# Twelve projection slots of a two-block network: high and low activations in one matmul of 512 columns, added on eviction

## The reference, cut to what matters

```python
for l in range(2):
    x = x + 0.5 * swiglu(rms_norm(x, norm_ffn1[l]), ffn1_wi[l], ffn1_wo[l])
    h = rms_norm(x, norm_mix[l])
    p = h @ w_in[l]                      # 1024 -> 2688 columns: the mixing slots
    p_a, p_q, p_k, p_v, p_c = jnp.split(p, split_pts, axis=-1)
    y_a, v_first = rwkv7_mixer(p_a, v_first, ...)
    y_b = chunk_attention(p_q, p_k, p_v, ...)
    y_c = multiscale_pool(p_c, ...)
    x = x + jnp.concatenate([y_a, y_b, y_c], axis=-1) @ w_out[l]
    # inside: q = rms_norm((h @ wq).reshape(B_, T, X_HEADS, X_HEAD_DIM), q_gain)
    x = x + memory_cross_attention(rms_norm(x, norm_cross[l]), ..., x_wq[l], ...)
    x = x + 0.5 * swiglu(rms_norm(x, norm_ffn2[l]), ffn2_wi[l], ffn2_wo[l])
```

## Time and profile before

| | |
|---|---|
| time, median of 3 runs | 2594.04 us (2592.91 to 2595.14) |
| the profiled execution | 2592.74 us |
| its span, first to last instruction | 2590.9 us |
| TensorE busy | 2297.9 us (89%) |
| VectorE busy | 1071.0 us (41%) |
| ScalarE busy | 855.4 us (33%) |
| GpSimd busy | 79.9 us (3%) |
| mean granted TensorE clock | 0.938 |

### The profile page before, as it was taken

One profiled execution on the slowest core, in us unless ns is written; L12 is line 12 of the kernel. 1 busy time (PEld: TensorE's weight loads), 2 busy tenths in 40 slices (PEclk: granted clock), 3 DMA queues, 4 the chain that ended last, 5 costly groups with the idle time before them and its releaser, 6 DMA issues.

```text
span 2590.9 us, 37292 instructions
## 1 busy us (share of the span) xinstructions
PE 2297.9 (89%) x15288; PEld 1635.1 (63%) x15288; DVE 1071.0 (41%) x1681; ACT 855.4 (33%) x1348; POOL 79.9 (3%) x87
## 2 busy tenths in 40 slices
PE   7998998777777777777779999999999999999999
PEld 7996494222323332232237889888888889888887
DVE  7867761000010000000005557756455547665554
ACT  4483141000010000000005445545445445545543
POOL 0000012000000000000000000100000000200000
PEclk9999999888788898878889999999999999999999
DMA  6434089999999999999995554043556554133553
GB/s 244 178 131 152 2 324 376 426 427 427 427 428 427 427 426 427 427 427 427 427 421 203 184 173 169 22 177 117 194 182 210 186 193 157 67 112 117 180 194 114
DMA packets 116818, 669.15 MB, mean 258 GB/s; under 512 B 10826, under 2 KB 14069, under 8 KB 56400
## 3 DMA queue, kind: packets, MB, share of 16 engines
q1 hardware_dynamic: 111376, 650.14, 64.2%
q0 software_dynamic: 3008, 12.96, 1.4%
q10 hardware_dynamic: 2304, 4.20, 0.4%
HBM read 662.01 MB, written 5.24 MB: 258 GB/s over the span
## 4 chain that ended last, share of the span: by engine, by line
PE 56%; DMA 27%; SPq 5%; DVE 4%; issue 3%; ACT 2%; DVEq 1%; POOLq 1%; ACTq 0%; POOL 0%
PE psd L694 22%; PE psd L688 10%; PE psx L694 9%; DMA scr<-in_w_up 8%; DMA ring<-in_w_down 7%; DMA hx<-in_w_down 6%; SPq L3183 5%; DMA ring<-in_w_gate 2%; DMA e_w_hi<-in_w_up 2%; PE psd L1097 2%; PE psx L1364 1%; PE psx L1112 1%; PE psx L938 1%; PE psd L1059 1%; DVE scr L2202 1%
## 5 line engine op out<-in xcount | busy, mean ns | idle before, releaser
L2202 DVE TENSOR_TENSOR w_lo<-ring,w_hi 128x1024 fp32r<-128x1024 f32 x436 | 515.9, 1221 | 392.4 <-ACT w_hi L1633 391.5
L1633 ACT ACTIVATE w_hi<-ring 128x1024 fp32r<-128x1024 f32 x436 | 437.2, 1048 | 478.0 <-PE psd L694 252.1
L694 PE MATMUL psd<-w_hi,h_cut 128*128 128x512 f32 x1536 | 481.5, 395 | 2.0 <-DVE h_cut L2202 1.6
L688 PE MATMUL psd<-h_cut,w_hi 128*128 128x256 f32 x1824 | 335.7, 287 | 11.7 <-DVE h_cut L2202 7.5
L694 PEld LDWEIGHTS psd<-w_hi,h_cut 128*128 128x128 f32 x1536 | 284.4, 189 | 59.5 <-DVE h_cut L2202 2.4
L694 PE MATMUL psd<-w_lo,h_cut 128*128 128x512 f32 x768 | 300.6, 391 | 0.0
L688 PEld LDWEIGHTS psd<-h_cut,w_hi 128*128 128x128 f32 x1824 | 286.9, 194 | 16.2 <-issue 13.5
L688 PE MATMUL psd<-h_cut,w_lo 128*128 128x256 f32 x912 | 259.7, 285 | 0.0
L1622 ACT ACTIVATE scr<-psd 128x512 f32<-128x512 f32 (+1 forms) x54 | 30.9, 573 | 572.8 <-PE psd L1075 360.6
L694 PE MATMUL psx<-w_hi,halves 128*128 128x512 f32 x704 | 218.2, 391 | 0.0
L2202 DVE TENSOR_TENSOR scr<-psd,scr 128x512 f32<-128x512 f32 (+1 forms) x24 | 15.9, 668 | 432.6 <-PE psd L1059 432.1
(11 more groups left out here) (411 smaller groups left out, 2905.5 us busy)
## 6 DMA issues: line engine op xcount, KB each, us to landing
ring<-in_ffn_wi SPq DMA_DIRECT2D x88, 1024.0 KB, 5.3
scr<-in_w_gate SPq DMA_DIRECT2D x48, 1024.0 KB, 26.6
scr<-in_w_down SPq DMA_DIRECT2D x48, 1024.0 KB, 26.2
scr<-in_w_up SPq DMA_DIRECT2D x48, 1024.0 KB, 26.8
ring<-in_ffn_wo SPq DMA_DIRECT2D x44, 1024.0 KB, 4.8
ring<-in_w_gate SPq DMA_DIRECT2D x32, 1024.0 KB, 26.6
ring<-in_w_up SPq DMA_DIRECT2D x32, 1024.0 KB, 26.7
ring<-in_w_down SPq DMA_DIRECT2D x32, 1024.0 KB, 26.5
```

The lines of the kernel that those rows point to most:

```text
L688: mm = pe.matmul(o, w[u], a[:, v, :], start=start and i == 0, stop=stop and i == 2, **kw)
L694: mm = pe.matmul(o, a[:, u, :], w[v], start=start and i == 0, stop=stop and i == 2)
L1633: act.activation(hi, src, ACT.Copy).then_inc(hi_cut, 1)
L2202: return dve.tensor_tensor(o, a, b, op)
```

## The change

In `mix_in` slots 6 to 9 and `x_q` slots 1 and 2 of either layer (twelve slots), `twin` takes the place of `dense`. It claims two banks, one for each tile m. One matmul of 512 columns takes the high weight tile against the high and low activations together and puts the two products into the two halves of the bank; a second one of 256 columns adds low weight by high activation to the first half. That is 2 x 8 x 2 = 32 matmuls. On eviction ScalarE copies the second halves of both banks out (`keep_low`), VectorE adds the first halves to them and then multiplies by `by_token` in place (`join`). `dense_plan` gets one more place for each of these slots. Nothing else is changed.

```diff
+TWINS = {"mix_in": (6, 7, 8, 9), "x_q": (1, 2)}
+def twin_count(key):
+    (part, l), i = key
+    both = [(p, n, j) for n in range(LAYERS) for p in ("mix_in", "x_q") for j in TWINS[p]]
+    return both.index((part, l, i)) + 1
...  dense_plan
-        plan += [((("mix_in", l), i), "dve") for i in range(11)]
+        for i in range(11):
+            plan += [((("mix_in", l), i, 0), "dve")] * (i in TWINS["mix_in"]) + [((("mix_in", l), i), "dve")]
...
+        for i in range(4):
+            plan += [((("x_q", l), i, 0), "dve")] * (i in TWINS["x_q"]) + [((("x_q", l), i), "dve")]
...  on TensorE
+            def twin(key, rhs):
+                banks = [DB.claim(pe, (*key, 0)), DB.claim(pe, key)]
+                w = cut(slot_of(key), k=KD)
+                for m in range(2):
+                    o = m2(banks[m])
+                    for k in range(KD):
+                        if (m, k) == (0, KD // 2):
+                            rest_cut(slot_of(key))
+                        hi, lo = [v[:, k, m * P:(m + 1) * P] for v in w]
+                        pe.matmul(o, hi, rhs[:, :, k, :], start=(k == 0), stop=False, skip_group_check=True)
+                        mm = pe.matmul(o[:, 0, :], lo, rhs[:, 0, k, :], start=False, stop=(k == KD - 1), skip_group_check=True)
+                mm.then_inc(slots_done, 1)
...
-                        dense((("mix_in", l), i))
+                        (twin if i in TWINS["mix_in"] else dense)((("mix_in", l), i), h_cut)
...  (x_q with mn_cut in the same way)
...  on ScalarE
+            def keep_low(key, to):
+                act.wait_ge(slots_done, slot_of(key) + 1)
+                for m, k in enumerate(((*key, 0), key)):
+                    ins = copy(to[:, 2 * key[1] + m, :], m2(DB.bank(k))[:, 1, :])
+                ins.then_inc(S("low_kept"), 1)
...
                 for i in range(11):
+                    if i in TWINS["mix_in"]:
+                        keep_low((("mix_in", l), i), pb)
                     cut_ahead(cutter, (("mix_in", l), i))
...  (x_q with xq in the same way)
...  on VectorE
+            def join(key, to):
+                two = slice(2 * key[1], 2 * key[1] + 2)
+                dve.wait_ge(S("low_kept"), twin_count(key))
+                for m, k in enumerate(((*key, 0), key)):
+                    j = two.start + m
+                    ins = tt_(to[:, j, :], m2(DB.bank(k))[:, 0, :], to[:, j, :], ALU.add)
+                dread(ins)
+                dve.drain()
+                dread(tt_(to[:, two, :], to[:, two, :], by_token, ALU.mult))
...
                 def project(i):
-                    b, m = m2(d_ready(dve, (("mix_in", l), i))), 2 if i < 10 else 1
-                    dread(tt_(pb[:, 2 * i:2 * i + m, :], b[:, 0:m, :], by_token[:, 0:m, :], ALU.mult))
+                    if i in TWINS["mix_in"]:
+                        join((("mix_in", l), i), pb)
+                    else:
+                        b, m = m2(d_ready(dve, (("mix_in", l), i))), 2 if i < 10 else 1
+                        dread(tt_(pb[:, 2 * i:2 * i + m, :], b[:, 0:m, :], by_token[:, 0:m, :], ALU.mult))
                     cut_ahead(cutter, (("mix_in", l), i))
```

More of the change, by code:

```diff
@@ L227, in dense_plan @@
         plan += [((("state", l), i), "dve") for i in range(4, STATES)]
-        for part, count, reader in (("mix_rows", 4, "dve"), ("x_q", 4, "dve"), ("x_rows", 4, "dve")):
-            plan += [(((part, l), i), reader) for i in range(count)]
+        plan += [((("mix_rows", l), i), "dve") for i in range(4)]
+        for i in range(4):
+            plan += [((("x_q", l), i, 0), "dve")] * (i in TWINS["x_q"]) + [((("x_q", l), i), "dve")]
+        plan += [((("x_rows", l), i), "dve") for i in range(4)]
         ffn(l, "ffn2")
@@ L1553, in _ @@
                     else:
-                        dense((("x_q", l), i), mn_cut)
+                        (twin if i in TWINS["x_q"] else dense)((("x_q", l), i), mn_cut)
                     if i == 1:
@@ L2164, in _ @@
                 for i in range(4):
+                    if i in TWINS["x_q"]:
+                        keep_low((("x_q", l), i), xq)
                     cut_ahead(cutter, (("x_q", l), i))
@@ L3027, in _ @@
                 for i in range(4):
-                    b = m2(d_ready(dve, (("x_q", l), i)))
-                    dread(tt_(xq[:, 2 * i:2 * i + 2, :], b, by_token, ALU.mult))
+                    if i in TWINS["x_q"]:
+                        join((("x_q", l), i), xq)
+                    else:
+                        b = m2(d_ready(dve, (("x_q", l), i)))
+                        dread(tt_(xq[:, 2 * i:2 * i + 2, :], b, by_token, ALU.mult))
                     cut_ahead(cutter, (("x_q", l), i))
```

## The result

The changed kernel takes 2605.17 us (median of 7 runs, 2599.56 to 2612.23) against 2593.75 before: ratio 1.0048, 95% interval 1.0038 to 1.0057, so 11.4 us slower. The forecast was 2597.4, in a range that ended at 2600.8: right about the sign, wrong about the size, and outside its range. The seven runs spread over 12.7 us, those of before over 2.2. The execution profiled took 2603.62 us, with a span of 2601.8.

What follows compares the result with a forecast made beforehand. The prediction took PE (TensorE) to bound the touched slots. Terms of +0.7, +1.2 and +1.5 gave +3.4 us on the profiled 2592.74, so 2596.1, and with 1.30 for the median 2597.4, range 2593.6 to 2600.8.

Steps and rivals of the forecast that it cites:

- Twin slot: On PE, each twin slot takes 5.55 us, 0.21 less than a dense one; twelve slots give -2.5 us.
- Join: Eviction of a twin slot by ScalarE copies, then VectorE adds and multiply: 2.15 us, 1.5 more than before.
- Layer 0 to mix_in 9: Behind mix_in 9 in layer 0 nothing covers the join: +1.5 less four slot gains, +0.7 us.
- Layer 1 behind mix_in 9: VectorE and GpSimd products go one after the other, making what follows late: +1.2 us, bounds -0.8 and +2.0.
- x_q, per layer: Ahead of x_q 2, PE waits 1.18 us for x_q 0's bank, less two slot gains: +0.76 us per layer.
- rival 3: VectorE becomes the bound of the slots, each join on the path: +15.5 us, 2609.5; chance 0.07.
- rival 4: Weight loads might not hide under 256-column products that follow 512-column ones: +23 and the 3.4, 2620 us; chance 0.03.
- the bound that it named: Layer 1 behind mix_in 9, upper bound: GpSimd goes ahead twice and slot 10's transposes are late too, +2.0 us.
- the sum: Layer 0 +0.7, layer 1 +1.2 and x_q +1.5 make +3.4 us, with PE's -2.5 in it.

Runs made afterwards that it cites:

- the fill: Kernel before with a twin in mix_in 9 only, plus 14 (layer 0) and 26 (layer 1) overwritten PE products behind slot 10: 2599.42 us, ratio 1.0023.
- the last experiment: Kernel before, all slots dense, with layer 1's value residual moved from GpSimd to VectorE ahead of slot 10's eviction: 2593.96 us, ratio 0.9997.
- the nine products more: Kernel before, all slots dense, with nine more products of 256 columns at the start of mix_in 2 in both layers: 2595.97 us, ratio 1.0006.
- x_q 1 and 2 alone: Kernel before with twins only in x_q slots 1 and 2 of both layers (four slots): 2595.63 us, ratio 0.9999.
- mix_in 9 alone: Kernel before with a twin only in mix_in slot 9 of both layers (two slots): 2602.58 us, ratio 1.0031.
- the change with the residual on VectorE: The changed kernel with layer 1's value residual moved from GpSimd to VectorE: 2601.45 us, ratio 1.0026 against the kernel before.

## Why the prediction was wrong

| Step | predicted, us | measured, us |
|---|---|---|
| Twin slot | 5.55 (-0.21) | 5.63 to 5.76 from start to start at the upper clock (-0.1 to -0.2) |
| Join | 2.15 | 2.15 |
| Layer 0 to mix_in 9 | +0.7 | +0.9 (1.3 less 0.4) |
| Layer 1 behind mix_in 9 | +1.2 | +1.5 by waits (2.9 less 1.4 of clock) |
| x_q, per layer | +0.76 | +1.28 and +1.25 |
| Lower clock | no term | +4.6 (1.5, 1.7, 1.4) |
| Gaps and rest of the solve of layer 0 | no term | +1.2 |

**Slots and join.** The join came out as written. The twelve slots gave some 1.6 us and not 2.5: a twin is 0.1 to 0.2 us shorter than the dense slot in its place. No PE wait stands ahead of mix_in 7 to 10: rival 3, VectorE as the bound of the slots, has nothing in the trace, nor has rival 4.

**Layer 1.** The size of the waits is near; the order is not. The prediction had VectorE and GpSimd take turns behind L2819; GpSimd came ahead of both products, which is the bound that it named. The meeting itself is shown by taking GpSimd's products away and by moving them. The Trainium skill ("SBUF — State Buffer", section "SBUF: two separate sides") lets whichever starts first keep the shared ports for its whole instruction, and the runs agree: 2.49 and 2.55 us beside GpSimd, 0.96 and 0.95 without it.

**x_q.** This step was mis-sized by 0.5 us in each layer. The wait was counted from 1730.00, the end of the row-scale products in the chain, but x_q 2 had begun at 1729.76: by starts it costs 1.48 us and not 1.18. And the two twins gave 0.2 together, not 0.42. The wait is also partly of `twin`'s making: it claims both banks ahead of its first product, though it writes the second only in the second half of the slot, some 2.8 us later. By these numbers a later claim would hide the 1.25 us; that is an estimate, and no run tests it.

**The step that failed** is the sum. It priced every product at the upper clock because the earlier trace rows read 1.00 in the slots, and took a wait at its own length. The waits and the slots' gain come to 4.9 us, 1.5 more than predicted; with them alone the time would have been 2598.9, inside the range. What took it out was 1.2 us of gaps and rest and 4.6 us of lower clock: PE ran at 1.2 GHz for 13.7 us from 1556 to 2585, where the trace of before has 3.4.

Behind mix_in 9 the term is shown to follow PE's idle time: the fill left the wait as it was, took the lower clock there away, and the trace's delay grew by 3.9 us less. The Trainium skill ("TensorE: Matmul & The Clock Gate", section "Part 1: The HAM clock gate") says the gate follows how busy PE has been lately and that the slow level is the default; those two stretches agree with that. In the trace of the change, though, only 1.4 of the 4.6 us stand there. The other 3.2 (mix_in 8 and the cross-attention of layer 0) stand behind work that is the same before, and the last experiment has both falls, with every slot dense and a median level with before; mix_in 8 of layer 1, dense, fell in two more. So it isn't shown that the change causes them. Nor does one trace of each kernel tell how much of the 4.6 us is the change and how much the execution: two kernels that are level with before (the nine products more, the residual on VectorE) have 13.7 us at the lower clock as well.

**Still open**: the gaps in the solves without a shown wait (0.5 to 1.9 us each), the falls other than those behind mix_in 9, and why x_q 1 and 2 alone leave the median where it was.

## What to carry to other kernels

A wait ahead of TensorE can cost more than its length, by what then runs at the lower clock behind it. Look for idle or thin work near the place and give the sum a term for it, with an upper end as large as the waits; and take more than one trace of a kernel before such a stretch is put down to a change. Before moving work on VectorE, ask which long product of GpSimd will then start first: here it started 0.17 us ahead, and two products of VectorE were held for 3.1 us in all. Fewer, wider products gain only the overhead of the ones removed, some 0.1 to 0.2 us a slot here, which a single eviction on the path takes back several times over.

## What the runs showed that was not expected

- Idle time of 3.60 us ahead of the transposes of layer 1 cost, besides itself, 1.4 us (the change) or 4.5 us (mix_in 9 alone) at the lower clock; 3.28 us of products with no use put there took it away at no cost to the wait. How long the clock stays low didn't follow from the wait: 3.4 us in the change, 13.7 with mix_in 9 alone, 10.2 with dense slots and a late eviction, all behind the same 3.60.
- A PE row that is busy for 6.00 of 6.00 us can stand at a granted clock of 0.72 (mix_in 8, twin or dense): 2.98 us of products of 32 rows had come before. The same products came in the trace before, without a fall.
- In layer 0, 2.16 us of idle time ahead of the transposes brought no lower clock in the change, but did with mix_in 9 alone, and did in the change with the residual on VectorE, whose layer 0 is the same: one wait, two prices.
